# Gate phase of an expert layer: seven early tiles from high and low parts, tiles in halves between gate steps, and a quarter of the gated one-hots on ScalarE

## The reference

```
q = (x @ wq).reshape(rows, 8 heads, 256)
s1, s2 = q[..., :128] . k1, q[..., 128:] . k2       # scores against 2 x 128 keys
...                                                 # top 16 of each, top 16 of their sums
experts = i1 * 128 + i2                             # 8 x 16 of 16384 experts for each row
g = softmax(sc)
hid = gelu(u_tab[experts] . x)
y = sum over experts of (g * hid) * v_tab[experts]
x = layer_norm(alpha * x + y)
```

## Time and profile before

| | |
|---|---|
| time, median of 3 runs | 1312.38 us (1312.07 to 1313.23) |
| profiled execution | 1311.79 us, span 1309.7 us |
| granted TensorE clock, mean | 0.992 |
| gate phase with hand-over | 550.9 to 675.9 us |
| main loop starts | 675.93 us |

### The profile page before, as it was taken

One profiled execution on the slowest core, in us unless ns is written; L12 is line 12 of the kernel. 1 busy time (PEld: TensorE's weight loads), 2 busy tenths in 40 slices (PEclk: granted clock), 3 DMA queues, 4 the chain that ended last, 5 costly groups with the idle time before them and its releaser, 6 DMA issues.

```text
span 1309.7 us, 25939 instructions
## 1 busy us (share of the span) xinstructions
PE 1267.6 (97%) x8435; PEld 1078.6 (82%) x8436; DVE 974.9 (74%) x2220; ACT 575.6 (44%) x1067; POOL 311.0 (24%) x521
## 2 busy tenths in 40 slices
PE   9999999889899999999999999999999999999996
PEld 6889888855555678799989988988988988988985
DVE  3666566276614699999988788788788888888886
ACT  4644666254421211133345445445445445445453
POOL 0003230400004588501122122122122222222201
PEclk9999999899899999999999999999999999999998
DMA  8655774579959687769859999999898998998962
GB/s 288 225 165 169 246 224 177 178 271 406 402 204 368 244 333 257 242 199 281 246 178 325 319 318 304 321 319 312 310 323 299 324 322 301 320 322 302 320 201 94
DMA packets 164383, 358.78 MB, mean 274 GB/s; under 512 B 49234, under 2 KB 99090, under 8 KB 160594
## 3 DMA queue, kind: packets, MB, share of 16 engines
q1 hardware_dynamic: 133410, 241.46, 54.3%
q0 software_dynamic: 25424, 111.37, 23.8%
q10 hardware_dynamic: 5472, 4.98, 1.2%
HBM read 341.56 MB, written 53.35 MB: 302 GB/s over the span
## 4 chain that ended last, share of the span: by engine, by line
PE 51%; DVE 4%; issue 2%; DVEq 1%; ACT 0%; POOLq 0%; POOL 0%; ACTq 0%
PE psum L1932 26%; PE psum L1921 7%; PE psum L1920 7%; PE psum L1919 7%; PE psum L1437 2%; PE psum L1941 2%; DVE gated_i L2099 2%; DVEq L2099 0%; DVE v_lo L2112 0%; DVE OT L2095 0%; ACT v_hi L2017 0%; DVE ln_bn L1364 0%; DVE x L1358 0%; DVE x L1387 0%; DVE gated_lo L2151 0%
## 5 line engine op out<-in xcount | busy, mean ns | idle before, releaser
L1921 PE MATMUL psum<-x_hi,u_lo 128*128 128x256 f32 x760 | 215.1, 283 | 0.0
L1920 PE MATMUL psum<-x_lo,u_hi 128*128 128x256 f32 x760 | 215.0, 283 | 0.0
L1919 PE MATMUL psum<-x_hi,u_hi 128*128 128x256 f32 x760 | 214.6, 282 | 0.0
L2112 DVE TENSOR_TENSOR v_lo<-big,v_hi 128x1024 fp32r<-128x1024 f32 x128 | 156.9, 1225 | 35.7 <-ACT v_hi L2017 34.0
L2017 ACT ACTIVATE v_hi<-big 128x1024 fp32r<-128x1024 f32 x128 | 135.4, 1057 | 84.6 <-PE psum L1932 83.4
L1932 PE MATMUL psum<-v_hi,gated_hi 128*128 128x512 f32 x504 | 157.0, 393 | 0.8 <-DVE gated_lo L2151 0.8
L1932 PE MATMUL psum<-v_lo,gated_hi 128*128 128x512 f32 x504 | 155.9, 390 | 0.0
L1932 PE MATMUL psum<-v_hi,gated_lo 128*128 128x512 f32 x504 | 155.6, 390 | 0.0
L1920 PEld LDWEIGHTS psum<-x_lo,u_hi 128*128 128x128 f32 x760 | 145.5, 191 | 3.7
L1919 PEld LDWEIGHTS psum<-x_hi,u_hi 128*128 128x128 f32 x760 | 145.5, 191 | 3.7
L1921 PEld LDWEIGHTS psum<-x_hi,u_lo 128*128 128x128 f32 x760 | 145.5, 191 | 0.0
(11 more groups left out here) (331 smaller groups left out, 2531.6 us busy)
## 6 DMA issues: line engine op xcount, KB each, us to landing
big<-in_peer_v SPq DMA_DIRECT2D x128, 512.0 KB
big<-in_peer_u SPq DMA_DIRECT2D x115, 512.0 KB, 5.2
w_then_a_vals<-in_a_v SPq DMA_DIRECT2D x8, 2048.0 KB
keep_ak<-in_a_k POOLq DMA_DIRECT2D x32, 508.0 KB, 5.9
keep_av<-in_a_v POOLq DMA_DIRECT2D x24, 512.0 KB, 5.6
big<-in_a_k SPq DMA_DIRECT2D x4, 2048.0 KB, 10.2
a_keys<-in_a_k SPq DMA_DIRECT2D x4, 2048.0 KB, 12.5
wq_ring<-in_peer_wq SPq DMA_DIRECT2D x16, 512.0 KB, 6.2
```

The source lines that it names most:

```text
L1919: pe.matmul(H[:, 0:SEQ], uh[:, q, kc], x1h[:, k, :], start=(k == 0), stop=False)
L1920: pe.matmul(H[:, 0:SEQ], uh[:, q, kc], x1l[:, k, :], start=False, stop=False)
L1921: mm = pe.matmul(H[:, 0:SEQ], ul[:, q, kc], x1h[:, k, :], start=False, stop=(k == KD - 1))
L2112: ve.tensor_tensor(vl[:, q], vs[:, q], vh[:, q].bitcast(F32), ALU.subtract).then_inc(s["v_lo"], 1)
```

## The change

Seven of the early tiles in the gate phase, n = 19, 21, ..., 31 (`SPLIT`), are computed from high and low parts: ScalarE copies the high part into `uh[1]` (`early_hi`), VectorE subtracts into `ul[1]` (`early_lo`), PE does 24 matmuls instead of 16. Every early tile after the first is cut into two halves, four of the eight pieces ahead of each gate step. ScalarE writes the last two (`BY_ACT`) of the eight gated one-hots of each step, as relu(gt - gt * |i1 - j|), which needs the negated gates `ngt`, computed once in the block before. The steps of VectorE are written out where they were a hardware loop. The second `u_hi` and `u_lo` move behind the last gate step, since `uh[1]` and `ul[1]` serve the early tiles until then. The early tile's write-out moves from even steps ahead of `W_out` to odd steps behind it. POOL's load of a tile waits for `hp_lo` where the tile two before is split.

```
 [route block, VectorE, last]
+            after(ve.tensor_scalar(t.ngt[:], gT[:], -1.0, None, ALU.mult))
...
+        SPLIT = [n for n in range(EARLY_R + 4, EARLY) if n % 2]
...
 [TensorE, gate_rows]
                 pe.wait_ge(s["onehot"], c + 1)
+                pe.wait_ge(s["onehot_act"], c + 1)
...
+            def early(n, parts):
+                if n in SPLIT:
+                    x = SPLIT.index(n)
+                    pe.wait_ge(s["hp_lo"], x + 1)
...
+                pe.wait_ge(s["hp_out"], n - 1)
+                out = bank(5 + 2 * (n % 2))[:, 0:SEQ]
+                for k in parts:
+                    kc = slice(k * P, (k + 1) * P)
+                    if n in SPLIT:
+                        pe.matmul(out, uh[:, 1, kc], x1h[:, k, :], start=(k == 0), stop=False)
+                        pe.matmul(out, uh[:, 1, kc], x1l[:, k, :], start=False, stop=False)
+                        mm = pe.matmul(out, ul[:, 1, kc], x1h[:, k, :], start=False, stop=(k == KD - 1))
+                    else:
+                        mm = pe.matmul(out, u[:, kc], t.xT[:, k, 0:SEQ], start=(k == 0), stop=(k == KD - 1))
...
                 for c in range(STEPS * g, STEPS * (g + 1)):
-                    if c % 2 == 0:
-                        early(EARLY_R + 1 + c // 2)
+                    early(EARLY_R + 1 + c // 2, range(KD // 2 * (c % 2), KD // 2 * (c % 2 + 1)))
                     gate_rows(c, c % 2)
...
 [ScalarE]
+            def early_hi(n):
+                x = SPLIT.index(n)
+                act.wait_ge(s[f"ld_e{n % 2}"], 16 * ((n - EARLY_R - 4) // 2 + 1))
+                if x:
+                    act.wait_ge(s["hp_mm"], n - 1)
+                act.activation(uh[:, 1], up[:, n % 2], ACT.Copy).then_inc(s["hp_hi"], 1)
+
+            def gated(c, q):
+                if c >= 2:
+                    act.wait_ge(s["c_mm"], c + 1)
+                for x in range(BY_ACT):
+                    r = c * GT + GT - BY_ACT + x
+                    ins = act.activation(dist[:, q, x], iof, ACT.Abs, bias=t.i1[:, r:r + 1], scale=-1.0)
+                ins.then_inc(s["act_dist"], 1)
+                act.wait_ge(s["act_dist"], c + 1)
+                for x in range(BY_ACT):
+                    r = c * GT + GT - BY_ACT + x
+                    ins = act.activation(A[:, q, GT - BY_ACT + x], dist[:, q, x], ACT.Relu, bias=t.gt[:, r:r + 1], scale=t.ngt[:, r:r + 1])
+                ins.then_inc(s["onehot_act"], 1)
+
+            act.wait_ge(s["iota_in"], 16)
+            for c in range(2):
+                gated(c, c)
...
                 for c in range(STEPS * g, STEPS * (g + 1)):
+                    W_out(c, g, GT * (c % STEPS), c % 2)
+                    if c + 2 < GROUPS * STEPS:
+                        gated(c + 2, c % 2)
                     if c % 2 == 0:
+                        if EARLY_R + 2 + c // 2 in SPLIT:
+                            early_hi(EARLY_R + 2 + c // 2)
+                    else:
                         early_out(act, d, t, s, EARLY_R + 1 + c // 2)
-                    W_out(c, g, GT * (c % STEPS), c % 2)
                 if g == 0:
                     u_hi(0, 16)
-                    u_hi(1, 16)
...
+            act.wait_ge(s["hp_mm"], EARLY)
+            u_hi(1, 16)
             hidden_early(0, 0)
...
 [VectorE]
-                for r in range(GT):
+                for r in range(GT - BY_ACT):
...
+            def early_lo(n):
+                x = SPLIT.index(n)
+                ve.wait_ge(s["hp_hi"], x + 1)
+                ve.tensor_tensor(ul[:, 1], up[:, n % 2], uh[:, 1].bitcast(F32), ALU.subtract).then_inc(s["hp_lo"], 1)
...
-                    with ve.Fori(0, STEPS // 4) as i:
-                        for q in range(2):
-                            onehots(i * 2 + (STEPS * g + STEPS // 2 * x + q), q)
+                    for c in range(STEPS * g + STEPS // 2 * x, STEPS * g + STEPS // 2 * (x + 1)):
+                        if c % 2 == 0 and EARLY_R + 1 + c // 2 in SPLIT:
+                            early_lo(EARLY_R + 1 + c // 2)
+                        onehots(c, c % 2)
...
                 if g == 1:
                     u_lo(0, 0)
-                    u_lo(1, 1)
+            u_lo(1, 1)
...
 [GpSimd]
-                if n >= EARLY_R + 6:
+                if n - 2 in SPLIT:
+                    gp.wait_ge(s["hp_lo"], SPLIT.index(n - 2) + 1)
+                elif n >= EARLY_R + 6:
                     gp.wait_ge(s["hp_mm"], n - 1)
```

More of the change, by code:

```diff
@@ L1787 @@
 GRP = 64
+BY_ACT = 2
 HWC = TILES * P
@@ L1819, in expert_block @@
         E = t.OT[:].rearrange("p k n -> p (k n)")[:, 0:2 * GT * NE].rearrange("p (s r j) -> p s r j", s=2, r=GT)
+        dist = t.OT[:].rearrange("p k n -> p (k n)")[:, 2 * GT * NE:2 * GT * NE + 2 * BY_ACT * P].rearrange("p (s r j) -> p s r j", s=2, r=BY_ACT)
         iof = t.big[:, BIG_IOTA:BIG_IOTA + P]
@@ L1942, in gate_rows @@
                 mm.then_inc(s["c_mm"], 1)
-            def early(n):
-                if n < EARLY_R + 4:
+            def early(n, parts):
+                if n in SPLIT:
+                    x = SPLIT.index(n)
+                    pe.wait_ge(s["hp_lo"], x + 1)
+                elif n < EARLY_R + 4:
                     pe.wait_ge(s[f"ld_p{n % 4}"], 16 * (n // 4 + 1))
-                    early_hidden(pe, t, s, n, t.big[:, n % 4 * D:(n % 4 + 1) * D])
+                    u = t.big[:, n % 4 * D:(n % 4 + 1) * D]
                 else:
                     pe.wait_ge(s[f"ld_e{n % 2}"], 16 * ((n - EARLY_R - 4) // 2 + 1))
-                    early_hidden(pe, t, s, n, up[:, n % 2])
-            early(EARLY_R)
+                    u = up[:, n % 2]
+                pe.wait_ge(s["hp_out"], n - 1)
[8 more added lines that the diff above has]
+                        mm = pe.matmul(out, u[:, kc], t.xT[:, k, 0:SEQ], start=(k == 0), stop=(k == KD - 1))
+                if parts[-1] == KD - 1:
+                    mm.then_inc(s["hp_mm"], 1)
+            early(EARLY_R, range(KD))
             for g in range(GROUPS):
                 for c in range(STEPS * g, STEPS * (g + 1)):
-                    if c % 2 == 0:
-                        early(EARLY_R + 1 + c // 2)
+                    early(EARLY_R + 1 + c // 2, range(KD // 2 * (c % 2), KD // 2 * (c % 2 + 1)))
                     gate_rows(c, c % 2)
@@ L2315 @@
 ld_wq3 ln_sum ln_st ln_mean ln_var ln_root ln_fac ln_scaled ln_lg
-ln_l ln_rg ln_r top topr topb top2 ixf be ber beb bei pr128 pair pair_v bf g_sub g_exp g_den g_fin id_eq id_mul id_sum
+ln_l ln_rg ln_r bei pr128 pair pair_v bf g_sub g_exp g_den g_fin id_eq id_mul id_sum
 id_turn id_out split y_done ld_u0 ld_u1 ld_v20 ld_v21 ld_ln2 y_low u_hi u_lo v_hi v_lo h_mm gelu hw hw_hi hw_lo y_mm c_mm
-W_out onehot zero iota_in st_y""".split()
-LATE_SEMS = """o_mm x_turn x_out x_hi x_lo q_mm q_out sc_mm sc_out x1_twice ld_g0 ld_g1 ld_g2 ld_g3 dots dots_kept n_gelu values st_w0 st_w1 ld_w0 ld_w1
-ld_p0 ld_p1 ld_p2 ld_p3 ld_e0 ld_e1 hp_mm hp_out st_h0 st_h1 ld_h0 ld_h1 gelu_p""".split()
+W_out zero iota_in st_y""".split()
+LATE_SEMS = """onehot onehot_act act_dist top topr topb top2 ixf be ber beb o_mm x_turn x_out x_hi x_lo q_mm q_out sc_mm sc_out x1_twice ld_g0 ld_g1 ld_g2 ld_g3 dots dots_kept n_gelu values st_w0 st_w1 ld_w0 ld_w1
+ld_p0 ld_p1 ld_p2 ld_p3 ld_e0 ld_e1 hp_mm hp_hi hp_lo hp_out st_h0 st_h1 ld_h0 ld_h1 gelu_p""".split()
 def build(nc, d, upto=9):
@@ L2398, in build @@
         t.sg = sb("sample_gates", [P, 64])
+        t.ngt = sb("gates_negated", [P, SEQ])
         route_block(nc, d, t, s)
```

## The result

The changed kernel takes 1332.94 us (median of 4, 1332.3 to 1335.73), the kernel before 1312.81: a ratio of 1.0153, 95% interval 1.0141 to 1.0165. The change makes it slower by 1.5%; 1332.0 was forecast. The profiled execution took 1332.3 us, its span is 1330.5, 20.8 more than before.

What follows compares the result with a forecast made beforehand. TensorE (PE), busy 97% of the span, was taken to bound the kernel. Stalls +19.4, split work -4.05, old waits -1.5 and hand-over +5.7 gave +19.6 us, median 1332.0; range 1320 to 1345.

Steps and rivals of the forecast that it cites:

- The new chain: Gate phase: early_hi behind W_out and gated, early_lo ahead of one-hots; 7.74 us against PE's 4.97, seven waits, +19.4 us.
- PE's work: Gate phase: seven early tiles become 24 matmuls at 0.12 us each, 4.05 us less for PE.
- the old waits: Gate phase: PE's 1.5 us of waits for one-hots goes, since VectorE loses 64 of them.
- The hand-over: Last gate step to main loop: late parts for product 1 and a fallen clock start the loop 5.7 us later.
- PE's chain: Hand-over: product 1 starts at 3.92 us, runs 5.1 at half pace, zero matmuls take 0.86; loop starts at 9.9.
- the second chain: Hand-over on SP: load_u(3, 5, 1) waits for u_lo(1), both first load_w queue behind it; first value matmul at 9.6 us.
- The start: Before the expert block: the extra negation costs VectorE 0.33 us, PE nothing, or 0.3 if not covered.
- The sum: Whole kernel: +19.4 - 4.05 - 1.5 + 5.7 = +19.6 us, median 1332.0; chance 0.66.
- The cheap chain: Rival, gate phase: gated takes 0.81 us, one-hots 0.20, clock stays up; +11.9 us, 1324; chance 0.10.
- The clock: Rival, gate phase: waits at split tiles drop PE's clock, 3.2 us each, 22 in all; 1354 us; chance 0.14.
- table load: Rival, ScalarE's one-hots: each use of gated loads a table for 1.28 us, 9 in all; 1341 us; chance 0.03.
- The case without a stall: Rival, split tiles: high part ready when PE arrives because pieces overlap; -2.05 us, 1310.3; chance 0.07.

Runs made afterwards that it cites:

- Experiments 1: Changed kernel with early_hi ahead of gated(c+2) on ScalarE in even steps instead of behind it: 1325.47 us, ratio 1.0093 to the kernel before.
- experiment 2: Changed kernel with early_hi one step earlier, behind gated in the odd step before: 1313.37 us, ratio 1.0005 to the kernel before.
- experiment 4: Changed kernel without split tiles, two versions: u_hi(1) and u_lo(1) back after steps 7 and 15, 1311.57 us; still behind the last gate step, 1315.73 us.
- experiment 6: Changed kernel with all eight gated one-hots on VectorE and none on ScalarE: 1329.45 us, ratio 1.0131 to the kernel before.
- experiment 7: Changed kernel with first load_w ahead of load_u(3, 5, 1), 18 zero matmuls before product 1, or both: 1334.51, 1333.30, 1331.37 us, one run each.
- SP's order alone: Changed kernel with the two first load_w ahead of load_u(3, 5, 1) on SP, no zero matmuls added: 1334.51 us, one run.

## Why the prediction was right

**The new chain** was the deciding step and held piece by piece. Forecast 7.74 us from the end of a gate step to the gate step after next, measured 7.6 at tile 31; Abs and Relu 0.395 and 0.495 long, measured 0.390 and 0.486, and `gated` 1.53, measured 1.50 (675.36 to 676.86 in ScalarE's timeline); six one-hots at 0.256, measured 1.55 for six: fixed addresses made them no faster. The forecast wait of 2.77 us per split tile is 19.4 us in all, and the weight loads' rows show 11.1 + 8.3 = 19.4. Experiments 1 and 2 show it as a matter of order alone: 10.4 and 20.2 us back without an instruction less.

**PE's work.** The 4.05 us of the split and the old waits are seen in experiment 2 (115.0 us against 115.2 of work), and the part without the split in experiment 4 (120.8 to 118.9). The two differ by 3.9 us.

**The hand-over** was forecast at 9.9 and measured at 9.7, but with the order of its two chains reversed: the gate tile took 3.3 us to land, not 2.8, and the clock stayed at half pace for a shorter time than product 1 lasts (granted 0.57 in 690 to 694; 4.3 us from its start to the zero matmuls instead of 5.1). PE's chain thus ended 9.2 us after the last gate step, and that the total is still right to 0.2 us is partly luck: the second chain, forecast at 9.6, took over. Which one ends last changes with the time at half pace: in experiments 2 and 6, with all of product 1 at half pace, it was PE's. That both chains lie within a microsecond was forecast, and experiment 7 shows it. Experiment 4 shows the whole loss alone, 4.9 us.

**The start** was forecast at nothing to 0.3 us and came 0.9 later. VectorE's negation is the last instruction ahead of the block, where PE was before. First the kernel before, then the changed one:

```profile
549.57 0.29 DVE L1782 COPY gates_of<-gates_turned 128x256 f32<-128x256 f32 x1
...
550.93 6.28 PE L1437 MATMUL psum<-x1T,big 128*128 128x256 f32 x28 [0.79 <-PEq L1456]
```

```profile
550.23 0.29 DVE L1782 COPY gates_of<-gates_turned 128x256 f32<-128x256 f32 x1
550.56 0.29 DVE L1783 TENSOR_SCALAR gates_negated<-gates_turned 128x256 f32<-128x256 f32 x1
...
551.83 5.49 PE L1969 MATMUL psum<-x1T,big 128*128 128x256 f32 x24 [1.03 <-DVEq L1456]
```

PE's idle time there grew from 0.79 to 1.03 us, so the negation cost at most 0.24. The copy just ahead of it, which the change does not touch, was already 0.66 us later; the start lay between 551.0 and 554.8 us in the profiles of the changed kernels, with the same code ahead of it.

**The sum.** Between the two profiles +20.8 us were measured and +19.6 forecast: +14.4 in the gate phase for 19.4 - 4.05 - 1.5 = 13.85, +5.5 in the hand-over for 5.7, and 0.9 at the start for nothing.

**The rivals.** The cheap chain fell with its prices (above). The clock did not fall in the gate phase: in the profile of the changed kernel it is 1.00 up to the hand-over, through fourteen waits of 1 to 1.9 us with 1.4 us of work or more between:

```profile
551.60:687.00 135.40, 118.45 (x864) 111.40 (x864) 105.17 (x249) 92.26 (x186) 19.71 (x25) 1.00 0.66 195
```

The Trainium skill ("TensorE: Matmul & The Clock Gate", section "A second HAM failure mode: psum-queue depth-cycling") tells of a kernel whose clock went up and down with short, frequent idle times; this trace does not show that for waits of this size. No table load stands among ScalarE's one-hots, before the Gelu table is loaded (once, at 622.3 us) or after. The Trainium skill ("ScalarE: Activation LUTs", section "Table sets: the hidden batching unit") has relu, copy and abs in every set, and the trace agrees. The case without a stall did not come about: from `W_out` to the one-hots no piece started more than 0.1 us before the end of the one ahead of it.

## What to carry to other kernels

Before a piece of work is handed to an idle engine, follow its place in that engine's order and in the order of the engine that takes it up: seven copies in the wrong slot cost 20 us on engines that were at most 75% busy in that stretch, and the same copies one step earlier cost PE nothing that the profile shows. Ask also what a reused buffer pushes behind the last step, and which loads are queued behind the wait that moves with it. Where two chains end close together, only an experiment that shortens both shows what either costs.

## What was not expected of the hardware

A wait of PE of 3.7 us was followed by half pace for a time that differed between profiles: product 1 took 4.3 us in the changed kernel, 5.3 in experiment 2 and with SP's order alone in experiment 7; why is open. 18 matmuls on zeros in the wait kept it at 3.0. The 64 KB gate tile landed 3.3 us after its issue, later than the 128 KB store's 2.8; a 512 KB load took 9.5 us during the gates' store, and 11.1 with another 512 KB load beside it.
